# A two-layer hybrid mixer trunk: the gate product in one short-format matmul a tile, and the small turns by VectorE's 32x32 transposes

## The reference

```python
h = rmsnorm(x, norm_g)
(qa, ka, va, ga, qb, kb, vb, ab, gb, cq, ckv, kr, gc, mg) = split_cols(h @ w_in)   # ab: 16 wide, kr: 32 wide
...
log_a = jax.nn.log_sigmoid((ab @ w_alpha + b_alpha).astype(jnp.float32)) / B_GATE_TAU
yb = gla_chunk_readout(..., log_a.reshape(B, S, B_HEADS, B_KEY_DIM))
...
k_rope = apply_rope(kr[:, :, None, :], cos_c, sin_c)[:, :, 0]      # shared by all heads of branch c
```

## Time and profile before

| | us |
|---|---|
| median of three runs | 930.22 (930.02 to 930.24) |
| the profiled execution | 930.3 |
| its span in the profile | 928.5 |
| PE busy in it | 920.6 (99%) |
| DVE busy | 603.7 (65%) |
| ACT busy | 389.3 (42%) |

### The profile page before, as it was taken

One profiled execution on the slowest core, in us unless ns is written; L12 is line 12 of the kernel. 1 busy time (PEld: TensorE's weight loads), 2 busy tenths in 40 slices (PEclk: granted clock), 3 DMA queues, 4 the chain that ended last, 5 costly groups with the idle time before them and its releaser, 6 DMA issues.

```text
span 928.5 us, 13090 instructions
## 1 busy us (share of the span) xinstructions
PE 920.6 (99%) x5108; PEld 754.6 (81%) x5108; DVE 603.7 (65%) x984; ACT 389.3 (42%) x727; POOL 0.2 (0%) x4
## 2 busy tenths in 40 slices
PE   9999999999999999999999999999999999999997
PEld 7988888888888777888889888888888887778886
DVE  7856467448756877575467764674477668876834
ACT  7453344324543454432344433442264425562324
POOL 0000000000000000000000000000000000000000
PEclk9999999999999999999999999999999999999999
DMA  7424324322434255422233333152235433454542
GB/s 292 136 72 146 114 69 137 113 92 81 141 121 141 83 150 148 147 92 91 91 114 91 105 100 107 65 174 98 91 94 145 136 114 109 122 156 136 148 125 90
DMA packets 43933, 110.98 MB, mean 120 GB/s; under 512 B 8608, under 2 KB 11552, under 8 KB 43744
## 3 DMA queue, kind: packets, MB, share of 16 engines
q1 hardware_dynamic: 39808, 104.82, 36.0%
q10 hardware_dynamic: 4064, 5.33, 2.2%
HBM read 85.41 MB, written 2.23 MB: 94 GB/s over the span
## 4 chain that ended last, share of the span: by engine, by line
PE 86%; DVE 5%; ACT 3%; SPq 2%; issue 1%; DMA 1%; ACTq 1%; DVEq 0%
PE ring L664 65%; PE nat L664 9%; PE nat L877 3%; PE aux L901 2%; SPq L501 1%; DVE w_lo L1229 1%; ACT work L1131 1%; PE nat L679 1%; PE nat L678 1%; PE nat L680 1%; DVE work L1531 1%; DMA raw<-pieces 1%; ACT w_hi L918 1%; PE ring L679 1%; PE ring L678 1%
## 5 line engine op out<-in xcount | busy, mean ns | idle before, releaser
L664 PE MATMUL ring<-act_hi,w_hi 128*128 128x512 f32 x784 | 308.8, 394 | 0.0
L664 PE MATMUL ring<-act_lo,w_hi 128*128 128x512 f32 x784 | 305.5, 390 | 0.0
L664 PE MATMUL ring<-act_hi,w_lo 128*128 128x512 f32 x784 | 305.3, 389 | 0.0
L918 ACT ACTIVATE w_hi<-raw 128x1024 fp32r<-128x1024 f32 x152 | 161.6, 1064 | 337.2 <-PE ring L664 271.9
L1229 DVE TENSOR_TENSOR w_lo<-raw,w_hi 128x1024 fp32r<-128x1024 f32 x152 | 184.7, 1216 | 82.5 <-ACT w_hi L918 82.3
L664 PEld LDWEIGHTS ring<-act_hi,w_hi 128*128 128x128 f32 x784 | 147.1, 188 | 38.3 <-issue 8.4
L664 PEld LDWEIGHTS ring<-act_hi,w_lo 128*128 128x128 f32 x784 | 147.2, 188 | 31.2
L664 PEld LDWEIGHTS ring<-act_lo,w_hi 128*128 128x128 f32 x784 | 147.2, 188 | 29.7
L1562 DVE SCALAR_TENSOR_TENSOR gates<-ring,rstd 128x512 f32<-128x512 f32 x72 | 49.4, 686 | 76.9 <-PE ring L664 76.8
L664 PE MATMUL ring<-y_hi,w_hi 128*128 128x512 f32 x192 | 74.9, 390 | 0.0
L664 PE MATMUL ring<-y_hi,w_lo 128*128 128x512 f32 x192 | 74.7, 389 | 0.0
(11 more groups left out here) (232 smaller groups left out, 1000.7 us busy)
## 6 DMA issues: line engine op xcount, KB each, us to landing
raw<-pieces SPq DMA_DIRECT2D x152, 512.0 KB, 3.5
bank_g<-work SPq DMA_DIRECT2D x120, 64.0 KB, 2.0
lat<-work SPq DMA_DIRECT2D x72, 64.0 KB, 2.0
bank_g<-work ACTq DMA_DIRECT2D x40, 64.0 KB, 2.2
xt<-x_t SPq DMA_DIRECT2D x8, 256.0 KB, 5.2
bank_a<-work SPq DMA_DIRECT2D x32, 64.0 KB, 2.0
bank_g<-bank_a SPq DMA_DIRECT2D x16, 128.0 KB, 3.9
out<-gates SPq DMA_DIRECT2D x7, 256.0 KB, 2.1
```

The costliest lines, as they stand in the source:

```text
L664: mm = pe.matmul(dst, stationary, moving, start=start and i == 0, stop=stop and i == 2)
L918: nc.scalar.activation(w_hi[:, n % HL, :], raw[:, n % RAW, :], ACT.Copy).then_inc(hi_split.sem, 1)
```

## The change

It has three parts.

- **Norms by token.** PE's four transposes (L782) go. DVE transposes 32 partitions at a time, four times 32x128 numbers, and copies a column (five instructions where one copy stood).
- **Gate input and rope key.** PE's four transposes (L788) go. DVE splits the gate input into a high part and a rest (two instructions on 128x64 numbers) and turns both, four transposes; then it turns the rope key, four transposes. ACT copies the turned block twice into `ab1`, each 32x512, in place of its two copies out of PSUM.
- **The gate product.** `alpha_all` is in the short format: its high part, made by ACT, and rows with the rest, made by DVE in two instructions of 32x512, once, in layer 0. Rows of `ab1` hold the high part and the rest of the input twice, so that one short-format matmul a tile sums the partial products. PE waits for `ab_doubled` in place of `ab_turned`, and for `alpha_lo_set`.

```diff
-AUX = [s for s in SCHEDULE if s[0] in ("rms", "rstd_nat", "gla_end", "latent", "turn_ab")]
+AUX = [s for s in SCHEDULE if s[0] in ("rms", "gla_end", "latent")]
...
-        alpha_all = sb("alpha_all", [P, DEPTH, B_HEADS * B_DK])
+        alpha_all = sb("alpha_all", [P, DEPTH, B_HEADS * B_DK], F32R)
...
+        ab1, ab_turn = y_hi[:, 2, :], merged[0:32, 4, :]
...
+        norm_t = gates[:, 7, 0:P].rearrange("p (t n) -> p t n", t=TT)
+        ab_nat = gates[:, 6, 0:P].rearrange("p (t n) -> p t n", t=TT).bitcast(F32R)
...
-                    elif name == "rstd_nat":
-                        aux_bank(layer, u)
-                        pe.wait_ge(rstd_set.sem, rstd_set.at(layer, 1))
-                        for t in range(TT):
-                            mm = pe.transpose(aux[:, t * P:(t + 1) * P], rstd[:, t * P:(t + 1) * P], ident)
-                    elif name == "turn_ab":
-
-                        aux_bank(layer, u)
-                        pe.wait_ge(k_ab_rot.sem, k_ab_rot.at(layer, 2))
-                        for t in range(TT):
-                            mm = pe.transpose(aux[0:48, t * P:(t + 1) * P], k_ab[:, t, :], ident)
                     elif name == "gla_gate":
 
-                        pe.wait_ge(ab_turned.sem, ab_turned.at(layer, 1))
+                        pe.wait_ge(ab_doubled.sem, ab_doubled.at(layer, 2))
+                        pe.wait_ge(alpha_lo_set.sem, 2)
                         pe.wait_ge(v_a_set.sem, v_a_set.at(layer, TT))
                         for t in range(TT):
                             mm = pe.matmul(nat_gate[:, t, :], ab1[:, t * P:(t + 1) * P], alpha_all[:, layer, :],
...
                     elif name == "early":
...
+                        if layer == 0:
+                            act.wait_ge(setup_loaded.sem, SETUP)
+                            nc.scalar.activation(alpha_all[:, :, :], alpha_raw, ACT.Copy).then_inc(alpha_hi_set.sem, 1)
                     elif name == "turn_ab":
-                        act.wait_ge(aux_ready.sem, aux_ready.at(layer, u + 1))
+                        act.wait_ge(ab_turned.sem, ab_turned.at(layer, 4))
                         act.wait_ge(ones_row.sem, ones_row.at(layer, 1))
-                        nc.scalar.activation(ab1[32:32 + B_RANK, :], aux[32:32 + B_RANK, :],
-                                             ACT.Copy).then_inc(ab_turned.sem, 1)
-                        nc.scalar.activation(k_rot, aux[0:C_ROPE, :], ACT.Copy).then_inc(aux_free.sem, 1)
+                        for rows in (slice(32, 64), slice(64, 96)):
+                            nc.scalar.activation(ab1[rows, :], ab_turn, ACT.Copy).then_inc(ab_doubled.sem, 1)
...
                         nc.vector.tensor_tensor(sq_sum, sq[0], sq[1], ALU.add).then_inc(lat_acc.sem, 1)
+                        if layer == 0:
+                            dve.wait_ge(alpha_hi_set.sem, 1)
+                            for rows in (slice(0, 32), slice(64, 96)):
+                                nc.vector.tensor_tensor(alpha_all[rows, :, :], alpha_raw[rows, :, :],
+                                                        alpha_all[rows, :, :].bitcast(F32), ALU.subtract).then_inc(alpha_lo_set.sem, 1)
...
                     elif name == "rstd_nat":
-                        dve.wait_ge(aux_ready.sem, aux_ready.at(layer, u + 1))
-                        nc.vector.tensor_copy(rstd_nat[:, :], aux[:, :].rearrange("p (t n) -> p t n", t=TT)[:, :, 0]
-                                              ).then_inc(aux_free.sem, 1)
+                        dve.wait_ge(rstd_set.sem, rstd_set.at(layer, 1))
+                        for q in range(4):
+                            rows = slice(32 * q, 32 * q + 32)
+                            nc.vector.transpose(norm_t[rows, :, :], rstd[rows, :].rearrange("p (t q n) -> p t q n", t=TT, q=4)[:, :, q, :]
+                                                ).then_inc(norm_turned.sem, 1)
+                        dve.wait_ge(norm_turned.sem, norm_turned.at(layer, 4))
+                        nc.vector.tensor_copy(rstd_nat[:, :], norm_t[:, :, 0]).then_inc(nat_norm.sem, 1)
+                    elif name == "turn_ab":
+                        dve.wait_ge(ab_split.sem, ab_split.at(layer, 2))
+                        ab_t = ab_turn.rearrange("p (t q n) -> p t q n", t=TT, q=4)
+                        k_t = k_rot.rearrange("p (t q n) -> p t q n", t=TT, q=4)
+                        for q in range(4):
+                            nc.vector.transpose(ab_t[:, :, q, :], ab_nat[32 * q:32 * q + 32, :, :].bitcast(F32)
+                                                ).then_inc(ab_turned.sem, 1)
+                        dve.wait_ge(k_ab_rot.sem, k_ab_rot.at(layer, 2))
+                        for q in range(4):
+                            nc.vector.transpose(k_t[:, :, q, :], k_ab[32 * q:32 * q + 32, :, 0:32]).then_inc(k_turned.sem, 1)
...
                             dve.wait_ge(k_ab_set.sem, k_ab_set.at(layer, TT))
+                            nc.vector.tensor_copy(ab_nat[:, :, 0:16], k_ab[:, :, 32:48]).then_inc(ab_split.sem, 1)
+                            dve.wait_ge(ab_split.sem, ab_split.at(layer, 1))
+                            nc.vector.tensor_tensor(ab_nat[:, :, 16:32], k_ab[:, :, 32:48], ab_nat[:, :, 0:16].bitcast(F32),
+                                                    ALU.subtract).then_inc(ab_split.sem, 1)
...
-    rows[32:32 + B_RANK] = w_alpha.transpose(1, 0, 2)
-    rows[32 + B_RANK] = b_alpha
+    for at in (32, 48, 64):
+        rows[at:at + B_RANK] = w_alpha.transpose(1, 0, 2)
+    rows[[0, 96]] = b_alpha
```

More of the change, by code:

```diff
@@ L350, in build_hybrid_trunk @@
         ones, ident = ones_r[:, :].bitcast(F32), con[:, IDENT:IDENT + P]
+        alpha_raw = bank_a[:, 2048 + P:2048 + P + DEPTH * 256].rearrange("p (l n) -> p l n", l=DEPTH)
         later, member = bank_a[:, 2048:2048 + P], con[:, MEMBER:MEMBER + 32]
@@ L373, in build_hybrid_trunk @@
         sq = [merged[:, 0, :], merged[:, 1, :]]
-        sq_sum, ln_ms, ab1, k_rot = merged[:, 2, :], merged[:, 3, :], merged[:, 4, :], merged[0:C_ROPE, 5, :]
+        sq_sum, ln_ms, k_rot = merged[:, 2, :], merged[:, 3, :], merged[0:C_ROPE, 5, :]
+        ab1, ab_turn = y_hi[:, 2, :], merged[0:32, 4, :]
         lat_rstd = merged[:, 6, :]
@@ L430, in build_hybrid_trunk @@
         ring_act = sig("ring_act", by_act(first_output(PIECES)))
-        k_ab_set, k_ab_prod, k_ab_rot, ab_turned = sig("k_ab_set", 4), sig("k_ab_prod", 4), sig("k_ab_rot", 2), sig("ab_turned", 1)
+        k_ab_set, k_ab_prod, k_ab_rot, ab_turned = sig("k_ab_set", 4), sig("k_ab_prod", 4), sig("k_ab_rot", 2), sig("ab_turned", 4)
+        norm_turned, nat_norm = sig("norm_turned", 4), sig("nat_norm", 1)
+        ab_split, ab_doubled, k_turned, alpha_hi_set, alpha_lo_set = sig("ab_split", 2), sig("ab_doubled", 2), sig("k_turned", 4), sig("alpha_hi_set", 0), sig("alpha_lo_set", 0)
         q_placed = sig("q_placed", 256)
@@ L519, in _ @@
             sp.dma_start(later, consts[:, LATER:CONSTS]).then_inc(setup_loaded.sem, 16)
-            sp.dma_start(alpha_all[:, :, :], alpha).then_inc(setup_loaded.sem, 16)
+            sp.dma_start(alpha_raw, alpha).then_inc(setup_loaded.sem, 16)
             for n in range(RAW + 1, DEPTH * PIECES):
@@ L1011, in _ @@
                         if p == PN1[3]:
-                            act.wait_ge(aux_free.sem, aux_free.at(layer, AUX.index(("rstd_nat", 0)) + 1))
+                            act.wait_ge(nat_norm.sem, nat_norm.at(layer, 1))
                             for t in range(TT):
@@ L1043, in _ @@
                             act.dma_start(v_as[64:128, :, :], v_a[0:64, :, :]).then_inc(v_shifted.sem, 16)
-                            act.wait_ge(aux_free.sem, aux_free.at(layer, AUX.index(("turn_ab", 0)) + 1))
+                            act.wait_ge(k_turned.sem, k_turned.at(layer, 4))
                             act.dma_start(k_rope_dram, k_rot).then_inc(k_rope_saved.sem, 16)
@@ L1316, in _ @@
                                                 ALU.mult).then_inc(sink_neg.sem, 1)
-                        nc.vector.memset(ab1, 1.0).then_inc(ones_row.sem, 1)
+                        nc.vector.memset(ab1.bitcast(F32), 1.0).then_inc(ones_row.sem, 1)
                         nc.vector.memset(v_as[0:64, 0, :], 0.0).then_inc(v_cleared.sem, 1)
@@ L1581, in _ @@
                             evacuated(layer, p)
-                            dve.wait_ge(aux_free.sem, aux_free.at(layer, AUX.index(("rstd_nat", 0)) + 1))
+                            dve.wait_ge(nat_norm.sem, nat_norm.at(layer, 1))
                             for t in range(TT):
```

## The result

| kernel | median us | executions | ratio to before (95% interval) |
|---|---|---|---|
| before | 930.31 | 8 | |
| changed | 933.00 (932.67 to 934.06) | 8 | 1.0030 (1.0021 to 1.0039) |

The change costs 2.7 us, 0.3%. The forecast was 931.7 (930.0 to 933.0); the median lies on the upper end of the range, and the sign at which "slower" begins (932.1) is passed.

What follows compares the result with a forecast made beforehand. PE's stream and the DVE and ACT chain to log_lo were taken to end together at gla_decay. With Abs 1.49 us later in layer 0 and 0.07 in layer 1, 930.3 + 1.56 gave a forecast of 931.7, range 930.0 to 933.0.

Steps and rivals of the forecast that it cites:

- the sign at which "slower" begins: Whole kernel: a time above 932.1 counts as slower, 0.2% or 1.9 us being what a measurement can tell; chance 32%.
- What bounds the kernel: At gla_decay, PE's stream and the ACT and DVE chain to log_lo end together; shortening PE alone gives nothing there.
- Rival A: PE's saving of 4.3 us is cashed in full, giving 926.0; chance 3%.
- rival B: DVE's additions cost nothing; piece 10's split, waiting for PE's piece 7, comes 0.89 us earlier a layer: 928.5; chance 5%.
- PE's side: Norm transposes 0.44, gate-input and rope-key transposes 0.45, gate product 1.25: 2.14 us a layer less on PE.
- DVE's side: Ahead of k_ab: cover 0.3 us, transposes 0.28 spaced 0.31, alpha 1.42; k_ab starts at 45.35 in layer 0, was 43.52.
- ACT's two copies: Copies of 32x512 into ab1 ahead of Abs: 0.61 us apart, with piece 10's split 0.52 behind the second.
- rival C: Small DVE transposes are dearer: at 0.345 us each the change costs 2.6 us, giving 932.8; chance 30%.
- C's sign: On DVE in the profile after: a transpose that takes 0.35 us or more.
- This wait of some 2.8 us (1.4 in layer 1) is not added: PE's wait at the gate product adds nothing to the total, since PE waits again at gla_decay.
- 36 matmuls of 0.228: PE's work behind the gate product in layer 0, after 0.48 us for the product; PE reaches gla_decay at 59.9.
- The range: Total of 930.0 to 933.0: all-overlap lower ends give 930.2; A and B lie below, C's worse tail half above.

Runs made afterwards that it cites:

- before_reordered: Kernel before with ACT's new order alone (Abs, Exp, Ln right behind turn_ab, split of piece 10 behind Ln, latent steps behind log_hi): 930.28 us, ratio 0.9999.
- act_first: both, with ACT's gate Abs, Exp, Ln right behind the ab1 copies, piece 10's split and latent steps later, DVE's latent-square rests behind log_lo: 926.95 us.
- best: act_first, with DVE's four rope_k instructions (2.84 us) moved from ahead of k_ab to behind piece 7: 925.79 us, ratio 0.9950.
- both: Changed kernel with alpha_all's split moved ahead of the norm and the gate input turned ahead of the split of weight piece 9: 928.83 us, ratio 0.9985.
- fill: Changed kernel with 12 unused short-format matmuls of 512 columns on PE ahead of the gate product, layer 0 alone: 932.65 us, ratio 1.0024.

## Why the prediction was off

- **What bounds the kernel** was right. `gla_decay` stood on two chains of equal length (before_reordered), and with less work on PE the one through DVE and ACT decided. Rival A's 926.0 needed a new order on ACT and DVE (act_first, best). `both` came near rival B's 928.5 without being held by B's bound.
- **PE's side**, 2.14 us a layer, was right: in `best` `gla_decay` comes 29.32 - 27.10 = 2.22 us earlier in each layer.
- **DVE's side** was right in kind: no cover ahead of `k_ab`, no overlap between transposes, alpha's two subtractions 1.42 us. The size of a transpose was 0.30, spaced 0.33, in place of 0.28 and 0.31: 0.08 us too little for each group of four, two groups a layer on the chain.
- **ACT's two copies**, with the start of the next instruction, took 1.30 in place of 0.61 + 0.52 = 1.13, which is 0.17 a layer. The 0.52 is the distance of full-width copies (L1007 at 50.51, L1008 at 51.03), which overlap; the instruction behind these two didn't overlap with them.
- These two terms, 2 x 0.08 + 0.17 = 0.33 a layer, are mis-sized. They make `log_lo` 1.80 and 0.40 us late instead of 1.49 and 0.07: 0.6 us of the error. The measured time is near rival C's 932.8, but not by C's mechanism: 0.02 us more for each of 16 transposes is 0.3 us, and C's sign, 0.35 or more for one, didn't appear.
- **The step that failed** is "This wait of some 2.8 us (1.4 in layer 1) is not added", with the "36 matmuls of 0.228" behind it, by which PE "reaches `gla_decay` at 59.9 and waits again". The wait itself was nearly right: 2.87 and 1.45 us measured, where the working gives 51.1 - 48.4 = 2.7 and the text says 2.8 and 2.7 in two places. But I took PE's pace behind it from rows in which PE had never stood still that long. Behind the wait of 2.87 us PE ran at half its clock: from the gate product at 51.22 to the matmul at 55.21 it took 3.99 us, where 0.57 + 8 x 0.228 = 2.39 would have done. Of these 1.6 us the slack ahead of `gla_decay` hid 0.9, and 0.7 were lost in the profiled execution; the wait ahead of `gla_decay` that the forecast had in layer 0 didn't occur, and came back when the fall was taken away (`fill`, 0.70 us). The Trainium skill, page TensorE: Matmul & The Clock Gate, Part 1, says that PE's clock has two levels and that idleness brings the lower. The trace agrees (0.50 in the stretch from 52 to 54 us), and I should have weighed it beside a forecast wait of that length.
- **The range** ended at 933.0 because it held only prices of the chain. The clock belonged in it as a cost above the sum.

## What to carry to other kernels

Where two chains end together, taking work from one of them is worth nothing until the other is shortened by an order of its own; here the same instructions gave 933.0 or 925.8 us by order alone. Ask of each helper engine not how busy it is but how much idle time it has directly ahead of the step that is waited for: DVE had 0.73 us there at 65% load, and 2.75 us were put ahead of it in layer 0 and 1.33 in layer 1. A new wait of PE of some 3 us is not free even where slack behind it seems to cover it, since the matmuls behind it may run at half the clock.

## What the runs showed of the hardware

- The granted clock was 0.50 for about 3 us behind waits of PE of 2.87 and 2.83 us, beginning 0.7 and 1.3 us after PE went on; behind waits of 1.45 and 1.7 us it stayed at 1.00. It seems not to fall in every execution: the mean clock of two of eight was 1.000, that of the others 0.996 or 0.997.
- A transpose of 32x128 numbers in float32 takes 0.30 us on DVE, and four that start in other partitions each time start 0.33 apart, without overlap, also where only the source's partitions change (L1379). That is as with L1353 and L1355 (0.68 long, 0.71 apart). Full-width transposes of 128x512 take 0.67 and do overlap: in the kernel before, two of L1531 stand 0.63 apart (228.25 and 228.88).
- Two copies of 32x512 on ACT (L1055) take 0.63 each and start 0.65 apart, with no overlap into the next instruction, where a full-width copy of 0.61 (L1003) is followed after 0.52. What makes the difference, the partitions or something else, wasn't tested.
- A short wait of PE costs more than its idle record: 0.57 us for a recorded 0.30 (act_first, layer 0).
